# Row scaling of the attention probabilities moved from VectorE to ScalarE

## The reference

```python
def one_block(qi):
    s = jnp.einsum('bqhgd,bkhd->bhgqk', qi, k).astype(jnp.float32) * scale
    p = jax.nn.softmax(s, axis=-1).astype(v.dtype)
    return jnp.einsum('bhgqk,bkhd->bqhgd', p, v)
```

## Time and profile before

| | us |
|---|---|
| median of 3 runs | 2778.53 |
| lowest, highest | 2771.99, 2784.85 |
| profiled execution, its own time | 2790.64 |
| its span (first to last instruction) | 2789.0 |
| TensorE busy | 2670.4 (96%) |
| VectorE busy | 1812.8 (65%) |
| ScalarE busy | 1138.4 (41%) |
| latent attention | about 180 to 360 us of the span |
| grouped-query attention | about 1076 to 1262 us of the span |

### The profile page before, as it was taken

The page is one execution under the profiler, slowest core; times in us unless marked ns, Lnnn a source line. Parts: engine busy times, 40 slices in busy tenths (PEclk is TensorE's granted clock), DMA queues, the critical chain, the costliest instruction groups (busy, mean ns, idle before and its releaser), DMA issues. The chain is left out here.

```text
span 2789.0 us, 38774 instructions
## 1 busy us (share of the span) xinstructions
PE 2670.4 (96%) x15262; PEld 2248.0 (81%) x15262; DVE 1812.8 (65%) x2902; ACT 1138.4 (41%) x1890; POOL 100.4 (4%) x123
## 2 busy tenths in 40 slices
PE   7989999999999999999999999999999999999997
PEld 4868887899999978888999978788767777778776
DVE  5568745666666666777888873656554656665666
ACT  3245535333333334555555532332233434333343
POOL 0110000100000000000000010000010000000000
PEclk9989999999999999999999999999989999999999
DMA  6430012433333311012333324222212222222221
GB/s 232 150 122 24 31 39 99 166 106 114 103 110 106 99 46 46 23 54 69 100 105 114 98 69 141 85 84 87 88 61 85 78 85 78 86 70 85 85 78 46
DMA packets 67261, 247.17 MB, mean 89 GB/s; under 512 B 7504, under 2 KB 7888, under 8 KB 66384
## 3 DMA queue, kind: packets, MB, share of 16 engines
q1 hardware_dynamic: 52144, 188.55, 20.6%
q0 software_dynamic: 14800, 55.65, 6.2%
q10 hardware_dynamic: 144, 0.52, 0.1%
HBM read 242.45 MB, written 2.24 MB: 88 GB/s over the span
## 5 line engine op out<-in xcount | busy, mean ns | idle before, releaser
L978 PE MATMUL PS<-HM,WH 128*128 128x512 f32 x1048 | 423.8, 404 | 10.4 <-DVE HM L2567 4.7
L2560 DVE TENSOR_TENSOR WL<-RAW,WH 128x1024 fp32r<-128x1024 f32 x199 | 243.4, 1224 | 273.9 <-ACT WH L1895 273.7
L979 PE MATMUL PS<-HM,WH 128*128 128x512 f32 x1048 | 415.6, 397 | 0.0
L980 PE MATMUL PS<-HM,WL 128*128 128x512 f32 x1048 | 415.3, 396 | 0.0
L978 PE MATMUL PS<-AB,BH 128*128 128x384 f32 (+1 forms) x1256 | 390.6, 311 | 6.5 <-DVE GATED L3074 3.7
L980 PE MATMUL PS<-AB,BL 128*128 128x384 f32 (+1 forms) x1256 | 388.2, 309 | 0.0
L979 PE MATMUL PS<-AB,BH 128*128 128x384 f32 (+1 forms) x1256 | 388.2, 309 | 0.0
L1895 ACT ACTIVATE WH<-RAW 128x1024 fp32r<-128x1024 f32 x199 | 209.7, 1055 | 285.7 <-PE PS L980 278.3
L978 PEld LDWEIGHTS PS<-HM,WH 128*128 128x128 f32 x1048 | 197.8, 189 | 67.2 <-issue 19.2
L978 PEld LDWEIGHTS PS<-AB,BH 128*128 128x128 f32 x1256 | 236.6, 188 | 12.5 <-DVE GATED L3074 7.1
L979 PEld LDWEIGHTS PS<-AB,BH 128*128 128x128 f32 x1256 | 236.7, 188 | 1.2 <-issue 0.5
(11 more groups left out here) (440 smaller groups left out, 5313.9 us busy)
## 6 DMA issues: line engine op xcount, KB each, us to landing
RAW<-in_tiles SPq DMA_DIRECT2D x299, 512.0 KB, 3.5
MRAW<-in_mods POOLq DMA_DIRECT2D x80, 512.0 KB, 4.8
RAW_M<-in_tiles SPq DMA_DIRECT2D x34, 512.0 KB, 3.5
TB<-bias_rows POOLq DMA_DIRECT2D x16, 576.0 KB, 6.3
FIRST<-in_mods SPq DMA_DIRECT2D x8, 1024.0 KB, 18.0
X_M<-in_x SPq DMA_DIRECT2D x1, 2048.0 KB, 13.1
VN_GB<-in_gm_rows POOLq DMA_DIRECT2D x2, 1024.0 KB, 6.0
out_x<-X_M SPq DMA_DIRECT2D x8, 256.0 KB, 2.1
```

Of the source, the lines that this page charges most:

```text
L978: pe.matmul(out_, wh, xh, start=first, stop=False, skip_group_check=True)
L979: pe.matmul(out_, wh, xl, start=False, stop=False, skip_group_check=True)
L980: return pe.matmul(out_, wl, xh, start=False, stop=last, skip_group_check=True)
L2560: dve.tensor_tensor(WL[:, s.mod(2), :], RAW[:, s.mod(2), :], f32(WH[:, s.mod(2), :]), ALU.subtract).then_inc(tile_split[s.mod(2)], 1)
```

## The change

ScalarE now does the multiplication, as a Copy activation whose scale is the reciprocal in `STAT`, and does it for step w + 1 as the first thing of turn w. VectorE makes the reciprocal only. The reciprocal stays where it was in VectorE's list. `row_prob` is now given by ScalarE, and ScalarE waits for `row_recip`; TensorE's list is the same.

```diff
@@ ScalarE, latent attention
+            def prob(w):
+
+                act.wait_ge(row_recip, w + 1)
+                st, at = STAT[:, w % 2, :], 0
+                for n, width in enumerate(mla_widths(w)):
+                    mm = copy(PROB[:, w % 2, at:at + width], PROB[:, w % 2, at:at + width], st[:, 4 + n:5 + n])
+                    at += width
+                mm.then_inc(row_prob, 1)
...
             exps(1)
+            prob(0)
             for w in range(MLA_UNITS):
                 j, n = w // MLA_STEPS, w % MLA_STEPS
+                if w + 1 < MLA_UNITS:
+                    prob(w + 1)
@@ ScalarE, grouped-query attention
+            def prob(w):
+
+                act.wait_ge(row_recip, GQA_W + w + 1)
+                copy(PROB[:, w % 2, :], PROB[:, w % 2, :], STAT[:, w % 2, 4:5]).then_inc(row_prob, 1)
...
             split(At(STREAM["gqa_q"] + 2), (gqa_v_done, 3))
+            prob(0)
             v_taken(2)
             for w in range(GQA_UNITS):
...
+                if w + 1 < GQA_UNITS:
+                    prob(w + 1)
                 pt_high_of(w)
@@ VectorE, latent attention
                 dve.reciprocal(st[:, 4:4 + n], st[:, 2:2 + n]).then_inc(row_recip, 1)
-                dve.wait_ge(row_recip, w + 1)
-                for m, width in enumerate(mla_widths(w)):
-                    ins = dve.tensor_scalar(PROB[:, w % 2, at:at + width], PROB[:, w % 2, at:at + width], st[:, 4 + m:5 + m], None, ALU.mult)
-                    at += width
-                ins.then_inc(row_prob, 1)
@@ VectorE, grouped-query attention
                 dve.reciprocal(st[:, 4:5], st[:, 2:3]).then_inc(row_recip, 1)
-                dve.wait_ge(row_recip, GQA_W + w + 1)
-                dve.tensor_scalar(PROB[:, w % 2, :], PROB[:, w % 2, :], st[:, 4:5], None, ALU.mult).then_inc(row_prob, 1)
```

More of the change, by code:

```diff
@@ L2892, in prob @@
                 dve.wait_ge(row_exp, w + 1)
-                st, n, at = STAT[:, w % 2, :], len(mla_widths(w)), 0
+                st, n = STAT[:, w % 2, :], len(mla_widths(w))
                 dve.reciprocal(st[:, 4:4 + n], st[:, 2:2 + n]).then_inc(row_recip, 1)
-                dve.wait_ge(row_recip, w + 1)
-                for m, width in enumerate(mla_widths(w)):
-                    ins = dve.tensor_scalar(PROB[:, w % 2, at:at + width], PROB[:, w % 2, at:at + width], st[:, 4 + m:5 + m], None, ALU.mult)
-                    at += width
-                ins.then_inc(row_prob, 1)
             def pt_low(w):
```

## The result

| | median, us | lowest, highest | runs |
|---|---|---|---|
| kernel before | 2779.64 | 2771.99, 2791.33 | 13 |
| changed kernel | 2798.19 | 2786.30, 2807.35 | 13 |

The changed kernel takes 1.0059 times as long (95% interval 1.0047 to 1.0072), which is some 16 us more (13 to 20); the two medians alone differ by 18.6. It is slower; 2801 was predicted. Its profiled execution took 2797.96 us, close to its median; that of before lay 11 us above its own median, so the two spans (2789.0 and 2796.3) differ by 7.3 us only.

What follows compares the result with a forecast made beforehand. TensorE was taken as the bound, VectorE's list setting the pace in part of a pair. Latent attention +14, grouped-query +5 and clock +4 made +23 us: 2801 us on the median of 2778.53, range 2778 to 2820.

Steps and rivals of the forecast that it cites:

- What bounds the kernel: Both attentions: TensorE is the bound, VectorE's list sets the pace in part of a pair; ScalarE has room by sum.
- The copy's price: ScalarE's multiplication: 930 ns for 768 columns, 509 for 256, adding 68 us of busy time; VectorE loses 45.
- The piece from reciprocal to low half: Latent attention: each such piece grows by 0.6 us (0.5 to 0.7), at n = 2 from 2.18 to 2.8.
- The path through the latent attention: Latent attention: pieces growing by 0.6 us, six per whole pair, plus the last steps, add 14 us (12 to 17).
- the last four steps: End of the latent attention: the multiplication ends 0.2 to 0.3 us after the transposes, adding 1.0 us.
- the last of the rivals: Both attentions: the clock falls in most turns, each pair losing two stretches more; 2814 to 2835 us, chance 0.14.
- 47.5 to 49 us for a pair: Sign that the forecast is right: a pair of heads in the latent attention takes this instead of 44.5 us.
- The clock: TensorE: two to three more holes per pair bring 2 to 3 more low-clock stretches, +4 us (0 to 10).
- The grouped-query attention: At the square roots the exponential starts 1.2 us late; three boundaries 4.3 us, 0.5 at the start: +5 us.
- Hidden: Rival: TensorE's backlog makes up its lag, only last steps and square roots count; 2778 to 2789 us, chance 0.21.
- the 0.15 us at 252.81: Transpose without listed hole, latent attention: its low half ended only 0.15 us before, so little slack absorbs the growth.
- The relief wins: Rival: multiplication over before the transposes land, needing the reciprocal 1.1 us ahead of their end; 2767 us, chance 0.08.

Runs made afterwards that it cites:

- e1: The change made in the latent attention only, the grouped-query attention as in the kernel before: ratio 1.0037 to the kernel before, latent attention 182.8 us.
- e3: The changed kernel with ScalarE's multiplication of row w + 1 moved just behind the high half of row w, both attentions: ratio 0.9982 to the kernel before.
- e2: The change made in the grouped-query attention only, the latent attention as in the kernel before: ratio 1.0008 to the kernel before.
- e6: The change in the latent attention only, with VectorE's reciprocal of w + 2 moved right behind the low half of w: ratio 0.9947 to the kernel before.
- e9: ScalarE multiplies behind the high half in the latent attention only, the grouped-query attention as in the kernel before: ratio 0.9964 to the kernel before.
- e10: Latent attention only: reciprocal early on VectorE and ScalarE's multiplication behind the high half; ratio 0.9979 to the kernel before.
- e12: The changed kernel with VectorE's reciprocal early, right behind the low half, in both attentions: 2768.34 us, ratio 0.9937 to the kernel before.
- e5: The kernel before with VectorE's multiplications left out in both attentions and nothing new on ScalarE: ratio 0.9921 to the kernel before.
- e11: The kernel before with VectorE's reciprocal and its own multiplication early in the latent attention, nothing moved to ScalarE: ratio 0.9979 to the kernel before.

## Why the prediction was right, point by point

**What bounds the kernel: right.** TensorE's waits for VectorE's low halves grew (11.7 to 15.7 us and 4.9 to 8.8), the pieces behind them set the length of a pair, and ScalarE's room by sum was worth nothing at the head of the turn: e1 to e3.

**The copy's price: right.** 936 and 501 ns for 930 and 509. ScalarE's busy time grew by 57 us only, for 68 said: the instructions overlap by 0.1 us, and busy time counts the overlap once. So did VectorE's fall by 41 for 45.

**The piece from reciprocal to low half: right in kind, a sixth too large.** It was put at 2.8 us for n = 2 and 2.2 for n = 4. The rows above give 2.59 and 2.10. Term by term for n = 2: 0.18 from reciprocal to multiplication (0.2), 0.85 to the next start (0.83), 0.26 for the output (0.3), 0.47 for the keys (0.5), and 0.83 from the high half's start to the low half's (0.81 and the rest of the handovers). Most of the difference is the last term: the copy of the row was taken at its whole length with a handover on top (0.81 and the better part of 0.15), and 0.83 is both together. Over the six pieces of this pair the growth is 0.41, 0.53, 0.51, 0.54, 0.41 and 0.69, mean 0.51 for the 0.6 taken.

**The path through the latent attention: 14 said, 12.8 measured, and partly by other terms.** The view of stretches, first of before, then of the changed kernel: three pairs of heads (each from the first transposes of its even head to those of the next), then head 6 with head 7 up to its second step, then the last four steps. Columns as in the earlier trace rows.

```profile
188.94:232.33 43.39, 40.26 (x279) 36.15 (x278) 35.67 (x64) 26.06 (x53) 0.00 (x0) 0.96 0.08 25
232.33:276.84 44.51, 41.21 (x297) 36.63 (x296) 36.15 (x65) 26.38 (x54) 0.00 (x0) 1.00 0.09 25
276.84:322.88 46.04, 42.74 (x298) 38.16 (x296) 36.14 (x65) 26.38 (x54) 0.00 (x0) 0.96 0.07 24
322.88:343.78 20.90, 18.02 (x123) 16.30 (x121) 16.70 (x29) 12.96 (x27) 0.00 (x0) 0.92 0.08 26
343.78:356.86 13.08, 10.26 (x77) 9.04 (x77) 10.26 (x16) 7.33 (x13) 0.00 (x0) 1.00 0.14 42
```

```profile
189.88:235.57 45.69, 39.47 (x279) 34.28 (x278) 30.66 (x52) 33.37 (x65) 0.00 (x0) 1.00 0.07 24
235.57:282.89 47.32, 41.56 (x297) 36.52 (x296) 30.83 (x52) 34.00 (x66) 0.00 (x0) 1.00 0.07 23
282.89:333.39 50.50, 45.66 (x297) 41.20 (x296) 30.84 (x52) 34.23 (x66) 0.00 (x0) 0.90 0.07 22
333.39:355.39 22.00, 18.04 (x122) 16.33 (x121) 13.93 (x23) 15.90 (x32) 0.00 (x0) 0.92 0.07 25
355.39:370.63 15.24, 11.68 (x77) 10.64 (x77) 7.87 (x12) 10.52 (x17) 0.00 (x0) 0.89 0.12 35
```

The second pair is the clean one, at full clock in both, so here the clock, the last of the rivals, has no part: 44.51 to 47.32, +2.8, where six pieces of 0.51 make 3.1 and 3.6 was predicted (47.5 to 49 us for a pair). The others are +2.3, +4.5, +1.1 and +2.2. Three pairs at 2.8, the 1.1 and the 1.0 that was said for the last four steps are 10.5. The other 2.3 are what the third pair (1.7) and the last steps (1.2), where the clock fell further than before, have on top, less 0.5 in the first pair.

**The clock: the right direction, some 3 us for 4.** In the latent attention, what is missing of full clock, length by (1 - granted clock), is 5.3 us in the rows of before and 8.5 in those of the change, 3.2 more. But not all of it reaches the end. The third pair of the changed kernel lacks 5.0 us (0.90) and is 3.2 longer than its second; that of before lacks 1.8 (0.96) and is 1.5 longer than its second. So the clock cost 1.7 us more in this pair and, with what the last steps show, some 2.3 in all. The grouped-query attention has another 1.0, below. Two things in it were not foreseen. e1 has the same clock as the change from the second pair on (1.00, 0.90, 0.92, 0.89) but 0.93 in the first, where the change has 1.00. And with the instructions of before, e2 ran its third pair at full clock:

```profile
278.01:322.53 44.52, 41.20 (x297) 36.63 (x296) 36.14 (x65) 26.41 (x54) 0.00 (x0) 1.00 0.07 24
```

So the same instructions take 44.5 or 46.0 us for a pair from one execution to another. In e6, e9, e10 and e12 the whole attention has a mean clock of 1.00, though their transposes wait from 8.6 us (e6) to 11.9 (e10) for low halves; in e5, with 6.3, it is 0.99. In which executions a hole is followed by a low stretch is not settled here: the holes of 2.30 and 0.78 us above were not. The Trainium skill ("Perfetto Trace Analysis", Matmul Optimizations) says that TensorE "dynamically scales power based on utilization". Before and the change agree with it in direction (a mean clock of 0.97 and 0.95 in this attention, with 15.4 and 24.3 us in which TensorE isn't busy); no run here says more.

**A wait that was not foreseen.** TensorE's value products now wait for ScalarE's taking of the output, `OA_M`, which stands behind the multiplication: 4.0 us in 4 waits. Of the 8.9 us that TensorE's idle time grew by in this attention, 4.0 are listed here and 4.0 at the low halves. They lie in stretches in which VectorE sets the pace, and the length of the clean pair leaves no room for a term of their own. With the doubled work it grows to 7.8.

**The grouped-query attention: the mechanism right, the sum 0.8 too large.** 5 was said, 4.2 measured with the late start. ScalarE behind the square roots in the changed kernel:

```profile
1128.04 0.94 ACT L1895 ACTIVATE PROB<-PROB,STAT 128x768 f32<-128x768 f32 x1 [1.53 <-DVE STAT L3294]
1128.88 0.79 ACT L1895 ACTIVATE PTA<-PS 128x768 fp32r<-128x768 f32 x1
1129.69 1.28 ACT L2324 ACT_TABLE_LOAD   x1
1130.99 0.99 ACT L2324 ACTIVATE PROB<-PS,STAT,LN 128x768 f32<-128x768 f32 x1
```

The reciprocal is at 1127.86, the exponential 3.13 us behind it; before it was 1119.39 - 1117.49 = 1.90. So 1.2 later, as said. The table load takes 1.28 us; that the prediction had 1.2 for it was luck. It took the wait of 1.21 us ahead of the exponential for the time of the load, but that wait is listed behind the load (1116.89 to 1118.17 in the trace of before, the exponential at 1119.39). And the transposes that had no hole at 1125.69 have one:

```profile
1137.00 0.85 PE L1564 MATMUL PS<-IDENT,PROB 128*128 128x128 f32 x6 [1.24 <-DVE PTA L2587]
```

From the transposes three turns ahead of it (1109.93 before, 1120.47 now) to these it takes 15.76 us before and 16.53 now, at the other two boundaries 15.42 and 16.53. So a boundary costs 1.1 us (0.8 at the first) where 1.4 was said: together 3.0 for 4.3. The exponential's 1.2 reach the transposes almost whole; the 0.2 added for the following piece doesn't show. At the start 0.2 is left for the 0.5 said: of the 1.1 us by which the first transposes are late, the next ones have made up 0.9. The last 1.0 is the clock's: behind the third boundary, where the hole is 3.56 us (2.40 before), the turn to the next transposes takes 10.66 us at a clock of 0.75, before 9.64 at 0.82. e2 has the same hole and 10.55 us.

**The sum.** 14 + 5 + 4 = 23 was said; 12.8 + 4.2 = 17.0 in the traces, some 16 by the ratio. By the prediction's own terms the latent pieces were 10.5 for 14, the grouped-query attention without the clock 3.2 for 5, the clock 3.3 for 4: each too large, the pieces by most. That 2801 lies only 3 us from the median of 2798 is in part luck: the two medians differ by 18.6 us, more than the ratio says, and the base of 2778.5 was 1 us under the median of the longer series.

**The rivals.** *Hidden* fell in the latent attention: the 0.15 us at 252.81 was no slack. In the grouped-query attention it held outside the boundaries: from a boundary's transposes to those five turns on it takes 25.9 us before and now. *The relief wins* fell for this order, at the point named: the reciprocal came too late. But its price was too low: 11 us, where the bound is 22 (e5), and moving the reciprocal gives 18 of it (e12). What the working lacked: it priced the relief at the 12 waits of TensorE in the earlier trace rows only. In e12 the clean pair takes 42.55 us instead of 44.51, and the mean clock of the attention is 1.00 instead of 0.97. The Trainium skill ("Perfetto Trace Analysis", Optimizing Scalar/DVE Operations) says that moving work to ScalarE may make sense where VectorE is saturated. The runs bound this: with VectorE at 78% it was worth -0.63% in one order (of which -0.21% is the order without any move, e11), and +0.59% in another, with the same instructions.

## What to carry to other kernels

An engine with room by its sum of busy time has room only at the places of its list where nobody waits behind. Before work is moved to such an engine, find the instruction on it that others wait for, and put the new work behind that one, or see to it that its input is there before the engine is. Here the same 80 instructions gave +0.6% at the head of the turn, -0.2% behind the high half, and -0.6% at the head with an early reciprocal. When the new work waits for a small result of the loaded engine (a reciprocal of 0.15 us), move that small result ahead of the loaded engine's long steps first, and check that what it needs in turn isn't queued behind the work just moved.

## What the runs showed of the hardware that was not expected

- Six activations of 128 columns cost 1.77 us from first start to the next instruction, one of 768 columns 0.85. By the two, an activation's start costs 0.18 us that no width removes ((1.77 - 0.85) / 5), and the other 0.67 us are the 768 columns. Four of 128 against two of 256 give the same 0.18 ((1.18 - 0.82) / 2).
- The same instructions of one pair of heads ran at a mean granted clock of 0.96 in one execution and 1.00 in another (before, e2), 46.04 and 44.52 us. A single trace can't tell a change of the clock of this size from chance.
